# Storing each expert's output rows with two DMAs of 64 rows in place of one DMA of two column halves

## What is computed

```python
def hier_moe(x, w_rg, b_rg, w_re, b_re, w_gate, w_up, w_down):
    ...
    gate = g_val * jax.nn.softmax(e_val, axis=-1)
    expert_id = g_idx * EXP_PER_GROUP + e_idx
    combine = jnp.sum(jax.nn.one_hot(expert_id, N_EXPERTS, dtype=F32) * gate[..., None], axis=1)

    def expert(acc, xs):
        wg, wu, wd, cw = xs
        h = jax.nn.silu(t @ wg) * (t @ wu)
        return acc + (h * cw[:, None]) @ wd, None
```

## Time and profile before

| | us |
|---|---|
| median of 3 runs | 2308.15 |
| lowest, highest | 2301.04, 2312.05 |
| span of the profiled execution | 2307.0 |
| main expert stage, layer 0 (first weight load issued to last copy done) | 844.66 to 1240.12 |
| main expert stage, layer 1 (the same) | 1862.07 to 2259.44 |

### The profile page before, as it was taken

The page is one execution under the profiler, slowest core; times in us unless marked ns, Lnnn a source line. Parts: engine busy times, 40 slices in busy tenths (PEclk is TensorE's granted clock), DMA queues, the critical chain, the costliest instruction groups (busy, mean ns, idle before and its releaser), DMA issues. The chain is left out here.

```text
span 2307.0 us, 23667 instructions
## 1 busy us (share of the span) xinstructions
PE 1611.7 (70%) x9141; PEld 1093.9 (47%) x9141; DVE 679.2 (29%) x1488; ACT 337.9 (15%) x887; POOL 111.9 (5%) x107
## 2 busy tenths in 40 slices
PE   6899958887869655555563799877779275655561
PEld 3786747776655432333231466544564243333330
DVE  3454036665340430010002353433230510000013
ACT  2242021111030100000001113222120000000001
POOL 0000011000300010000001000000000100000001
PEclk9899868888578877787877799989889687777776
DMA  7521110001225267686773303023223576767753
GB/s 253 125 89 41 37 41 1 1 1 44 64 82 203 109 222 263 253 299 227 289 257 114 112 26 137 1 91 137 74 87 150 191 258 226 287 252 263 267 191 142
DMA packets 107803, 340.82 MB, mean 148 GB/s; under 512 B 14407, under 2 KB 42671, under 8 KB 89743
## 3 DMA queue, kind: packets, MB, share of 16 engines
q1 hardware_dynamic: 92098, 284.04, 34.6%
q0 software_dynamic: 7296, 38.80, 4.6%
q10 hardware_dynamic: 8320, 16.78, 1.9%
HBM read 301.42 MB, written 38.17 MB: 147 GB/s over the span
## 5 line engine op out<-in xcount | busy, mean ns | idle before, releaser
L1707 PE MATMUL pp<-ring,uT 128*64 128x512 f32 x512 | 178.7, 834 | 312.0 <-ACT uT L1738 312.0
L1688 PE MATMUL pp<-ring,uT 128*64 128x256 f32 x2048 | 266.8, 405 | 1.6 <-DVE uT L1714 1.6
L1707 PEld LDWEIGHTS pp<-ring,uT 128*64 128x64 f32 x512 | 45.8, 176 | 386.7 <-issue 381.8
L1688 PEld LDWEIGHTS pp<-ring,uT 128*64 128x64 f32 x2048 | 160.8, 149 | 121.1 <-issue 64.4
L543 PE MATMUL pp<-uT,ring 128*128 128x272 f32 x576 | 137.7, 398 | 11.8 <-PEq L339 11.8
L1720 DVE TENSOR_TENSOR uT<-uT,pp 128x128 f32<-128x128 f32 x64 | 18.4, 288 | 430.4 <-ACT uT L1731 430.4
L1738 ACT ACTIVATE uT<-pp 128x512 f32<-128x512 f32 x64 | 38.2, 597 | 645.3 <-DMA expert_rows<-uT 633.9
L543 PEld LDWEIGHTS pp<-uT,ring 128*128 128x128 f32 x576 | 109.8, 193 | 34.0 <-issue 11.9
L1386 PE MATMUL pp<-ring,uT 128*128 128x512 f32 x256 | 115.9, 616 | 3.8 <-PEq L125 3.8
L1676 PE MATMUL pp<-consts,scaled_rows 64*128 64x64 f32 x512 | 70.1, 278 | 49.7 <-DMA scaled_rows<-sorted_rows 49.7
L1725 DVE COPY uT<-pp 128x128 f32<-128x128 f32 x64 | 18.7, 292 | 245.9 <-PE pp L1698 245.9
(11 more groups left out here) (551 smaller groups left out, 2414.6 us busy)
## 6 DMA issues: line engine op xcount, KB each, us to landing
ring<-in_w_exp_gate SPq DMA_DIRECT2D x64, 1024.0 KB, 7.0
ring<-in_w_exp_up SPq DMA_DIRECT2D x64, 1024.0 KB, 9.2
ring<-in_w_exp_down SPq DMA_DIRECT2D x64, 1024.0 KB, 15.8
scaled_rows<-sorted_rows SPq DMA_DIRECT2D x64, 256.0 KB, 14.8
expert_rows<-uT ACTq DMA_DIRECT2D x64, 256.0 KB
ring<-in_w_in_a SPq DMA_DIRECT2D x4, 3072.0 KB, 11.0
expert_rows<-zero_rows SPq DMA_DIRECT2D x2, 2176.0 KB
x<-in_x_prompt SPq DMA_DIRECT2D x2, 2048.0 KB, 11.0
```

The source lines that it names most:

```text
L1688: ins = TE.matmul(pp[0][q * SLOTS:(q + 1) * SLOTS, b * 512:b * 512 + 2 * P], xT[b][:, j, :], w[:, :, j, q * P:(q + 1) * P], start=(j == 0) ...
L1707: ins = TE.matmul(pp[2][q * SLOTS:(q + 1) * SLOTS, 0:512], hT[b][:, j, :], w[:, j, q * 512:(q + 1) * 512], start=(j == 0), stop=(j == 1))
```

## The change

The store of an expert's 64 rows is issued as two DMAs. Before, one DMA had the access pattern 2 x 64 x 512: the outermost dimension of the DRAM side is the column half q, then the 64 rows t, then 512 columns. Now each half q has a DMA of its own, from 64 partitions of `yr[b]` to 64 rows of 512 columns, with the rows outermost. Bytes, contiguous pieces (2 KB) and addresses are the same. The semaphore counts of `s.st` double throughout: 32 for each store.

```diff
@@ credits @@
                         for st in s.st:
-                            act.sem_inc(st, 16)
+                            act.sem_inc(st, 32)
@@ store @@
-                    act.wait_ge(s.st[b], 16 * n + 16)
+                    act.wait_ge(s.st[b], 32 * n + 32)
                     act.activation(yr[b][:], pp[2][:, 0:512], ACT.Copy).then_inc(s.y, 1)
                     act.wait_ge(s.y, e + 2)
-                    act.dma_start(dst.rearrange("t (q n) -> q t n", q=2), yr[b][:]).then_inc(s.st[b], 16)
+                    for q in range(2):
+                        act.dma_start(dst[:, q * 512:(q + 1) * 512], yr[b][q * SLOTS:(q + 1) * SLOTS, :]).then_inc(s.st[b], 16)
@@ end of the main stage @@
-                            act.wait_ge(main.st[b], 16 + 16 * NE // 2)
+                            act.wait_ge(main.st[b], 32 + 32 * NE // 2)
@@ the lane for experts with over 64 rows @@
-                                act.wait_ge(over.st[0], j * 16 + 32)
+                                act.wait_ge(over.st[0], j * 32 + 64)
```

## The result

The changed kernel takes 2119.47 us (median of 4 runs, 2109.10 to 2126.68), against 2306.18 us for the kernel before in the same comparison: a ratio of 0.919, 95% interval 0.916 to 0.922. It is faster by 187 us, where 275 were forecast. The profiled execution is the fastest of the four: its span is 2107.3 us, 200 us under that of before.

A forecast was written before the change was run, and what follows sets the result against it. Two full DMA engines were taken to bound the expert stages; with stores spread, DMA bytes would bind at 403 GB/s. Savings of 133.7 + 135.7 + 6 = 275 us from the 2307.0 us span gave 2033 us, range 2008 to 2085.

The forecast's parts named there:

- The bound before: Expert stages: two DMA engines carrying loads and stores are full, 423 us on each against the 396 us there are.
- The store spreads: Stores of expert rows: 64 rows outermost use 16 engines instead of two, q10 getting about 10240 packets.
- The rival that splitting is useless: Stores: they do not spread or spreading does not matter; 2308 us, no change; chance 0.03.
- the slower one: Stores stay on two engines and ACT's second issue delays the silu: up to 38 us more, 2346; chance 0.03.
- DMA as the next bound: Expert stages after the change: DMA bytes set the pace, 248 us until the last expert's rows are in.
- The rival with PE's clock: Expert stages: PE binds at mean clock 0.78, 2061 us; chance 0.24 for 2050 to 2090, shared with a slow DMA rate.
- the rate: DMA in the expert stages: 403 GB/s with weights, rows and stores mixed, 99.3 MB in 246 us.
- the sum: Each expert stage: 248 us until the last rows are in, plus 13.7 us to the last copy.
- The sign of being wrong: Mixed stretches of the stages: a rate under 380 GB/s would mean writes on all engines cost more than taken.
- The upper end: DMA time of a stage: 273 us, or 366 GB/s, from packet times including all waiting; 2083 us in all.
- The end of a stage: From the last copy to the landing of the last stores: 3 us gained for each layer, 6 in all.
- the tail from the last rows to the last copy: End of each expert stage: the last copy ends 13.7 us after the last expert's rows are there.

The follow-up runs named there:

- e6_spread2: Changed kernel with its two DMAs for each store each given an outermost dimension of 2, so each on 2 engines: layer 0 stage 395.8 us, whole 2313.1 us.
- e2_rows_128: Changed kernel with each expert's rows loaded to 128 partitions of 2 KB instead of 64 of 4 KB, results wrong: stage 258.0 us, whole 2006.1 us.
- e7_rows128_right: Changed kernel with rows loaded to 128 partitions and turned by 16 matmuls, results right: stage 257.7 us, whole 2017.32 us, ratio 0.876 to the kernel before.
- e4_no_stores: Changed kernel without the stores of the experts' rows in the main stages: layer 0 stage 295.9 us; whole time not comparable.
- e1_no_rows: Changed kernel without all but the first five row loads of each layer and PE's waits for them: layer 0 stage 234.0 us, whole 1970.9 us.
- e10_rows_step2: Changed kernel with the 64 rows loaded to every second of 128 partitions instead of partitions 0 to 63: stage 255.6 us, whole 2015.7 us.

## Why the prediction was right and where it was wrong

- **The bound before** (two full DMA engines) was right. With 2 and 4 engines for each DMA, the engines that carry stores are full by their packet times (423 of 396 us and 341 of 336).
- **The store spreads** as forecast: 10240 packets, no copy waits for a store any more. The rival that splitting is useless has fallen, by the same runs, though the two halves gain nothing where they stay on two engines (e6_spread2). So has the slower one: ACT's two issues did not hold PE up. PE waited 1.1 us in all for the copies, and these wait for the down product only (112.1 us in 64 places over the whole program).
- **DMA as the next bound** was right: PE waits for rows, DMA is at a share of 1.01. The rival with PE's clock has fallen: the waits did bring the mean clock down to 0.83, but PE was busy for 223 of 287 us and waited for the rest.
- **The term that failed is the rate**, "I take 403 GB/s, because it is the one stretch with the same mixture at full use". 99.3 MB took 291 us, 341 GB/s. The stretch of the earlier trace rows was 7 us long, shorter than a step of the new bound, and it ended where a dip began (1018 to 1020). What the runs showed in its place is a cost that the sum had at nothing: each row load into partitions 0 to 63 takes 1.8 us more than its bytes need, 48 us for the 27 of a stage. With 291 us the sum would have read 291 + 13.7 = 305 us for the stage (measured 306.3). With the dips removed (e2_rows_128, e7_rows128_right) the stage takes 258 us, 4 under the 262 of the sum: the forecast was that of a kernel without the dips.
- **How much of this could be read before.** Not all. The 353 GB/s of the stretch from 845 to 861 in the earlier trace rows is no such rate, since the loads were only beginning in its first 2 us (74 and 172 GB/s). With full engines and dips the kernel before had 380 GB/s over 25 us and 366 over 10, which by the same sum make 263 and 273 us in place of 248: 15 to 25 of the 43 us. The rest came with the change, since the dips cost more in it (47 us of each engine against 20); why is open.
- **The miss in numbers.** The stages were forecast at 248 + 13.7 = 262 us and took 306.3 and 310.4: 45 and 49 us too short, less 8 us won at their ends, are 86. The profiled execution lies 75 us over its forecast of 2032, because 10 us went outside the stages, where none were forecast. The median lies 86 us over 2033; that this is the same 86 is chance, as the profiled execution is the fastest of the four.
- **The sign of being wrong** came up, a rate under 380 GB/s, but with the wrong cause beside it: it was to mean that the writes on all engines cost more. Without the stores the dips are there (e4_no_stores), and without the row loads the rate is over 410 GB/s with the stores (e1_no_rows).
- **The upper end** had the right idea, packet times that include all the waiting, and the wrong number: 273 us against 291. It took the packets to be as long after the change as before it. But q1's packets took 252 us on each engine before, and 0.936 x 287 = 269 us for less data (91.04 MB against 92.02) after. Full engines by themselves do not lengthen them: with the rows in 128 partitions it is 2.44 us for each MB with full engines and 2.52 with part of them idle. The growth goes with the row loads into partitions 0 to 63.
- **The end of a stage** was taken at 3 us; it gave 6.6 and 7.0, because the last store lands and the block closes 5.5 us after the last copy, not 12.2. On the other side the tail from the last rows to the last copy took 15.3 us, not 13.7, since PE came to it at the low clock: the next half of `gate_up` took 3.60 us there, 1.95 in the earlier trace rows.

## What to carry to other kernels

A DMA whose outermost dimension is small is carried by few engines, however many bytes it has; look at how many small packets it leaves and at the rate when nothing else runs, and ask whether those few engines are full. When the bound moves to bandwidth, take the rate over at least one whole period of the new schedule, and look inside the period for stretches in which the engines are busy and the bytes are few. Loads that fill partitions 0 to 63 alone slowed all the loads around them here; filling all 128 (258.0 us) or every second one (255.6 us) did not.

## What the runs showed of the hardware that was not expected

Row loads of 7% of the bytes cost 24% of the stage (72 of 306 us) as long as they filled partitions 0 to 63, and 24 us (258.0 - 234.0) once they filled all. During such a load all the transfers of the changed kernel fell from 410 to some 270 GB/s with every DMA engine busy (share 1.02). DMA reads and writes of DRAM mixed on all 16 engines kept 415 to 417 GB/s over 230 us (e2_rows_128, e7_rows128_right, e10_rows_step2), as much as weight loads alone, 414.
